# A two-part model in one fp32 kernel: start, modulation rows, scan outputs and gated heads rearranged

## The chip, the cores and the metric

The kernel runs on one core of a Trainium2 chip. The metric is the time of one execution on the device in microseconds (us); lower is better. All matrix products are fp32.

## The reference, cut to what matters

256 tokens of width 1024 go through a first block (two layers: projection, convolution, windowed attention, layer norms; a dense feed-forward in layer 0, eight experts with two chosen a token in layer 1), and then through a second block of two layers with attention and a two-directional recurrent scan. What the change touches:

```python
h = layer_norm(x, ln_in_g, ln_in_b)                       # the start
mod_x = split(silu(c) @ w_ada[l] + b_ada[l], 3)           # modulation rows, c and c_ctx: 2 rows
mod_c = split(silu(c_ctx) @ w_ada[l] + b_ada[l], 3)
# the scan, per chunk of 128 tokens, for 4 heads and 2 directions
num = w_inter * (C @ q) + qk @ v
h = num / max(abs(den), exp(-m_t))                        # output of a chunk
C = a * C + (w * v) @ k                                   # state change
# the gated heads
h = rmsnorm(sigmoid(o_pre) * h) * head_g * silu(z)
out = concat([att, h]) @ w_out
```

## The kernel before, in words

Activations lie feature-major (128 features on the partitions, 8 chunks, 256 tokens along the free axis). TensorE (PE) does all products, VectorE (DVE) and ScalarE (ACT) what lies between, SyncE (SP) starts every transfer. Each engine has its own instruction list in program order, written out by hand in `build`; semaphores join them. Weights arrive as units of 1 MB (`next_unit`), into a ring of six slots before the experts; SP loads a unit as soon as PE has released the slot. PSUM has eight banks: `fill` makes PE wait until the last reader of a bank is done, `tile` makes a reader wait until PE has filled it.

The start. SP (lines 1521 to 1523) starts a transfer of the first constants (ones, identity, zeros and small ones), of the tokens `x_t` into `xc`, and of the parameters. PE waits for the constants, does two products of 128x512 whose results nobody reads (`spin(2)`), waits for the tokens, and sums them over the features with the matrix of ones (`norm_mean`); DVE subtracts the mean (L2090), ACT squares (L1597), PE sums the squares (`norm_var`), ACT takes the root (L1583), DVE scales (L2104, L2121) and PE takes up the projections after `spin(3)`.

The modulation rows. `w_ada` has 12 units a layer. For each, `condition_rows` or `condition_row` multiplies the two conditions, padded to 32 columns, with the unit's eight feature chunks: 16 fp32 products of 128x32 weights in 4 column groups of PE for every two units, chunk c in group c % 4, so that a row is spread over four groups of partitions. ACT copies the bank, and `condition_turns` (by `turn`) sums the four parts and turns them to feature-major with products against two columns of the constant `fold`: 2 of them a unit, 4 for two units. Ten of these pairs stand in the rounds of the first block's attention (`block1_attention`: six in layer 0, four in layer 1), where the order of each round is: scores, values of the round before, rows, half of the output projection, turns, transposes of the softmax (L689). Four units, two pairs, stand beside the norm at the end of layer 0 (`norm_beside_conditions`).

The scan (`mlstm`, on PE and on DVE). There are four steps j, in each both directions d. PE does for a step: scores of both directions, `inter(j,0)`, `state_change(j,0)`, `inter(j,1)`, `intra(j,0)`, `state_change(j,1)`, `intra(j,1)`, with pieces of projections between them (`mlstm_beside_projections`). `inter` and `intra` of both directions use the same two banks, 5 and 6: `intra(j,1)` waits until DVE's `output(j,0)` has taken its sum out of them (L2804, semaphore `mh_num`). DVE's own order in a step ends with `state_change(j,0)`, `state_change(j,1)` (L2792), `output(j,0)`, `output(j,1)` (L2804 to L2819). In layer 0 all four steps have outputs, in layer 1 the last two; the last step has no state change.

The gated heads (`mlstm_post` on DVE, `mlstm_turn`, `block2_out_start` and `block2_out` on PE). After the norm, PE transposes the heads of each tile of 128 tokens (L1429, 4 tiles in layer 0, 2 in layer 1, a bank each), and DVE multiplies each 128x128 piece by the gate (L2872 in layer 0, tile by tile; L2863 in layer 1, head by head). In layer 0 PE then waits for all four tiles before the second half of the output product; in layer 1 it waits head by head, and does the first half of another column chunk before that.

Of the kernel before, what the change touches and what calls it, by code (L numbers as in the profile page):

```python
# [14 lines left out]
P = 128  # L15
T = 256
# [162 lines left out]
def const_columns():  # L179
    c = Columns()  # L180
    for name, n in (("ones", P), ("ident", P), ("zeros", P), ("tri_f", P), ("eps5", 1), ("eps6", 1), ("one", 1), ("fold", COL),
                    ("tri_b", P), ("mask_f", P), ("mask_b", P), ("rot", P), ("cos", T), ("sin", T), ("win_mask", TT * 2 * T), ("slot", BIG), ("capacity", EXPERTS), ("bases", EXPERTS),
                    ("nbr_mask", TT * T), ("before", EXPERTS * EXPERTS)):
        c.add(name, n)
    c.early = c.at["eps5"][0] + 3 + COL
    return c
# [5 lines left out]
def build(nc, weights, params, consts, x_t, ctx_t, p_t, rel, out, rows_dram):  # L192
    with ExitStack() as ctx:
# [58 lines left out]
        row_of = (cond_row, other_row)  # L252
# [78 lines left out]
        names = """weights_used ones_loaded x_loaded params_loaded late_loaded rel_loaded rel_ready out_stored  # L331
# [118 lines left out]
        def _(eng):  # L450
# [32 lines left out]
            def spin(n):  # L483

                for _ in range(n):
                    mm(ps[:, 7, :], ones, con[:, 0:512], True, True)
# [94 lines left out]
            def row_products(l, u, o):  # L581
                w = next_unit()
                for c in range(KC):
                    at = 32 * (c % 4)
                    last = mm(o[at:at + 32, 0:GW], cond_s[:, c, :], w[:, c * GW:(c + 1) * GW], c < 4, c >= KC - 4)
                return last

            def condition_row(l, u, bank):
                o = fill(("row", l, u), bank, (s["cond_row"], UNITS_ADA * l + u + 1))
                row_products(l, u, o).then_inc(bank_full[bank], 1)  # L590

            def turn(u, rows, mod_t):
                for half in range(2):
                    at = 2 * (2 * u + half)
                    last = mm(mod_t[:, at:at + 2], rows[:, u % 2, half * P:half * P + P],
                              con[:, CN("fold", 0, 2)], True, True)
                return last

            def condition_turn(l, u, mod_t):
                eng.wait_ge(s["cond_row"], UNITS_ADA * l + u + 1)  # L600
                return turn(u, cond_row, mod_t)

            def condition_rows(l, n, beside=False):

                u = l * ADA_EARLY + 2 * n
                bank = 1 if n else 5
                o = fill(("row", l, u), bank, (s["cond_row"], UNITS_ADA * l + u + 2))
                for k in range(2):
                    w = next_unit(beside=beside or k == 1)
                    for c in range(KC):  # L610
                        at = 32 * (c % 4)
                        last = mm(o[at:at + 32, k * GW:(k + 1) * GW], cond_s[:, c, :], w[:, c * GW:(c + 1) * GW],
                                  c < 4, c >= KC - 4)
                last.then_inc(bank_full[bank], 1)

            def condition_turns(l, n, mod_t):
                u = l * ADA_EARLY + 2 * n
                eng.wait_ge(s["cond_row"], UNITS_ADA * l + u + 2)
                for k in range(2):
                    last = turn(u + k, row_of[n % 2], mod_t)  # L620
                if u + 2 == UNITS_ADA:
                    last.then_inc(bank_full[0], 1)

            def norm_beside_conditions():
# [8 lines left out]
                condition_row(1, 2, 7)  # L633
                condition_row(1, 3, 4)
                condition_turn(1, 2, mod_t)
                condition_turn(1, 3, mod_t).then_inc(bank_full[5], 1)
# [787 lines left out]
            def mlstm_turn(l):  # L1424
                eng.wait_ge(s["mh_normed"], l + 1)
                for t in range(4 if l == 0 else 2):
                    o = fill(("mt", l, t), t, (s["mh_mixed"], 8 if l else t + 1))
# [4 lines left out]
            def out_half(l, w, c, o, half):  # L1432
                alone = l == 1 and c >= CC
                n = 2 * T if l == 0 else T
                for k in range(CC * half, CC * half + CC):
                    if l == 1 and c == 0 and half == 1:
                        eng.wait_ge(s["mh_mixed"], 4 + k - CC + 1)
# [20 lines left out]
            def block2_out(l, started):  # L1458
                if l == 0:
                    eng.wait_ge(s["mh_mixed"], 4)  # L1460
# [116 lines left out]
        def _(eng):  # L1577
# [26 lines left out]
            def condition_row(l, u):  # L1604
                o = tile(eng, "row", l, u)
                eng.activation(cond_row[:, u % 2, :], o[:, 0:GW], ACT.Copy).then_inc(s["cond_row"], 1)

            def condition_rows(l, n):
                u = l * ADA_EARLY + 2 * n
                o = tile(eng, "row", l, u)  # L1610
                eng.activation(row_of[n % 2].rearrange("p a b -> p (a b)"), o, ACT.Copy).then_inc(s["cond_row"], 2)
# [417 lines left out]
            eng.wait_ge(s["ones_loaded"], 16)  # L2029
            norm("in", KC, T)  # L2030
            eng.wait_ge(s["params_loaded"], 16)
            eng.wait_ge(s["prep_done"], 1)
            eng.activation(cond_s[:, :, 0:2], par[:, PC.all("cond")].rearrange("p (c e) -> p c e", e=2), ACT.Silu)\
                .then_inc(s["cond_ready"], 1)
            for l in range(DEPTH):
# [11 lines left out]
                else:  # L2047
                    ffn()
                    condition_row(1, 0)
# [1169 lines left out]
```

## Time and profile before

| | us |
|---|---|
| median of 3 runs | 2022.15 (2021.82 to 2023.66) |
| the profiled execution, its own time | 2021.61 |
| its span, first to last instruction | 2019.8 |
| PE busy | 1979.9 (98%) |
| DVE busy | 754.0 (37%) |
| ACT busy | 404.1 (20%) |

The span of 2019.8 us lies within an execution of 2021.61 us; 1.8 us lie around it. An instruction row of the trace gives its start and its duration in us from the span's start, the engine, the line in the kernel, what it writes and reads, and how many instructions were merged; in brackets the idle time of the engine before it and what ended it. A fp32 product shows as two MATMUL records, a transpose as one. Ends of products are modelled, so durations of a merged row reach past the start of the next: pitch is read from starts. Rows of a view by shape give the count, then busy time, mean ns of one, and idle time before.

### The profile page before, as it was taken

How to read it: one execution, taken by the hardware profiler on the slowest of the kernel's cores; microseconds unless marked ns; L12 is line 12 of the kernel's file. 1: busy time of each engine (PE TensorE's matmuls, PEld its weight loads, DVE VectorE, ACT ScalarE, POOL GpSimd, SP SyncE). 2: the span in 40 equal slices, each digit the busy share in tenths (PEclk: the TensorE clock that was granted, in tenths of full speed). 3: DMA queues.
4: the chain of work that ended last, by engine and by line, in shares of the span. 5: the costliest groups of instructions: out<-in, count | busy, mean ns of one | idle time of the engine just before them, and what ended most of it. 6: DMA issues, size and time to landing. Idle time of an engine off the chain costs nothing.

```text
span 2019.8 us, 36525 instructions
## 1 busy us (share of the span) xinstructions
PE 1979.9 (98%) x15702; PEld 1439.5 (71%) x15702; DVE 754.0 (37%) x1781; ACT 404.1 (20%) x947; POOL 0.2 (0%) x4
## 2 busy tenths in 40 slices
PE   9999999999999999999999999999999999999998
PEld 7879999988766656666656666656755667566787
DVE  6847555587521111111111111111326823426725
ACT  1233110114310111000100010000214432223342
POOL 0000000000000000000000000000000000000000
PEclk9999999999999999999999999999999999999999
DMA  9473645455199999999999999999132111122220
GB/s 337 167 287 129 211 172 193 174 188 188 63 402 420 421 419 421 420 420 420 420 421 420 420 416 420 420 420 421 71 112 87 52 63 42 63 103 85 105 84 22
DMA packets 75826, 510.94 MB, mean 253 GB/s; under 512 B 7888, under 2 KB 14096, under 8 KB 14992
## 3 DMA queue, kind: packets, MB, share of 16 engines
q1 hardware_dynamic: 75664, 508.58, 63.0%
q8 instruction: 126, 2.06, 0.4%
q14 instruction: 36, 0.29, 0.0%
HBM read 507.46 MB, written 1.08 MB: 252 GB/s over the span
## 4 chain that ended last, share of the span: by engine, by line
PE 92%; DMA 4%; DVE 2%; ACT 1%; issue 1%; SPq 0%; DVEq 0%; ACTq 0%
PE ps L477 90%; DMA ring<-weights 3%; DMA work<-weights 1%; PE ps L1269 1%; PE ps L818 1%; PE ps L689 0%; SPq L1534 0%; DVE work L2872 0%; DVE work L2792 0%; DVE spare L2725 0%; DMA con<-consts 0%; DVE work L2116 0%; ACT work L1597 0%; DVE work L2804 0%; DVE small L2908 0%
## 5 line engine op out<-in xcount | busy, mean ns | idle before, releaser
L477 PE MATMUL ps<-work 128*32 128x256 f32 (+8 forms) x4912 | 516.6, 375 | 10.7 <-DVE work L2804 6.3
L477 PE MATMUL ps<-work,ring 128*128 128x256 f32 (+2 forms) x1992 | 503.7, 407 | 3.1 <-DVE work L2872 3.1
L477 PEld LDWEIGHTS ps<-work 128*32 128x32 f32 (+3 forms) x4912 | 345.3, 142 | 142.2 <-issue 77.0
L477 PEld LDWEIGHTS ps<-work,ring 128*128 128x128 f32 x1992 | 340.0, 191 | 137.5 <-issue 108.5
L477 PE MATMUL ps<-ring,work 128*32 128x256 f32 (+3 forms) x4392 | 405.8, 407 | 3.6 <-DMA ring<-weights 3.0
L477 PEld LDWEIGHTS ps<-ring,work 128*32 128x32 f32 (+1 forms) x4392 | 234.1, 120 | 130.2 <-issue 59.7
L477 PE MATMUL ps<-xc,ring 128*128 128x256 f32 (+1 forms) x1344 | 252.3, 348 | 0.0
L477 PEld LDWEIGHTS ps<-xc,ring 128*128 128x128 f32 x1344 | 222.7, 191 | 31.0 <-issue 5.1
L2378 DVE TENSOR_TENSOR work<-work,ps 128x256 f32<-128x256 f32 x42 | 17.7, 421 | 413.2 <-ACT work L1745 413.2
L1745 ACT ACTIVATE work<-ps 128x256 f32<-128x256 f32 x42 | 16.1, 384 | 557.8 <-PE ps L477 557.8
L477 PE MATMUL ps<-spare,work 128*32 128x256 f32 (+1 forms) x1128 | 120.4, 427 | 2.1 <-issue 1.2
L477 PE MATMUL ps<-xc,work 128*128 128x256 f32 (+1 forms) x624 | 117.2, 346 | 0.0
L477 PEld LDWEIGHTS ps<-xc,work 128*128 128x128 f32 x624 | 102.7, 191 | 16.3 <-issue 4.2
L2153 DVE SCALAR_TENSOR_TENSOR work<-work,par 128x256 f32<-128x256 f32 x240 | 98.0, 479 | 0.9
L2341 DVE TENSOR_TENSOR work<-ps,work 128x512 f32<-128x512 f32 x68 | 47.0, 691 | 92.4 <-PE ps L477 92.1
L477 PEld LDWEIGHTS ps<-spare,work 128*32 128x32 f32 x1128 | 52.2, 110 | 37.9 <-issue 21.2
L477 PE MATMUL ps<-work,con 128*128 128x256 f32 x230 | 55.4, 385 | 8.5 <-ACT work L1597 4.3
L477 PEld LDWEIGHTS ps<-work,con 128*128 128x128 f32 x230 | 42.2, 190 | 20.2 <-issue 8.2
L2499 DVE TENSOR_TENSOR work<-ring 128x512 f32<-128x512 f32 x52 | 33.6, 687 | 53.4 <-PE ps L477 53.4
L2392 DVE TENSOR_TENSOR work<-work 128x512 f32<-128x512 f32 x14 | 9.7, 692 | 97.6 <-ACT work L1751 97.6
L477 PE MATMUL ps<-xc,spare 128*128 128x256 f32 x192 | 42.7, 381 | 0.0
L477 PEld LDWEIGHTS ps<-xc,spare 128*128 128x128 f32 x192 | 36.2, 190 | 7.3 <-issue 1.7
(287 smaller groups left out, 1267.0 us busy)
## 6 DMA issues: line engine op xcount, KB each, us to landing
ring<-weights SPq DMA_DIRECT2D x287, 1024.0 KB, 15.0
work<-weights SPq DMA_DIRECT2D x130, 1024.0 KB, 20.3
spare<-weights SPq DMA_DIRECT2D x54, 1024.0 KB, 19.9
work<-rel SPq DMA_DIRECT2D x8, 512.0 KB, 13.6
spare<-rows SPq DMA_DIRECT2D x2, 2048.0 KB, 9.3
con<-consts SPq DMA_DIRECT2D x1, 1368.0 KB, 21.6
xc<-x_t SPq DMA_DIRECT2D x1, 1024.0 KB, 5.7
xc<-ctx_t SPq DMA_DIRECT2D x1, 1024.0 KB, 27.0
```

The source lines that it names most:

```text
L477: ins = eng.matmul(o, lhs, rhs, start=start, stop=stop, **kw)
L818: last = eng.transpose(o[:, k * P:k * P + P], pair_a[:, n % 2, k * P:k * P + P], ident)
L1269: last = eng.transpose(o[:, kt * P:kt * P + P], prob2_flat[:, at:at + P], ident)
L1745: eng.activation(pair_s[:, n % 2, :], o[:, 0:GW], ACT.Silu).then_inc(s["pair_silu"], 1)
L2153: ins = eng.scalar_tensor_tensor(out=conv_acc[:, j, :], in0=src, scalar=w, in1=conv_acc[:, j, :], op0=ALU.mult, op1=ALU.add)
L2341: return eng.tensor_tensor(r, o.rearrange("p (a b) -> p a b", b=T), r, ALU.add)
L2378: eng.tensor_tensor(pair_a[:, n % 2, :], pair_s[:, n % 2, :], o[:, GW:2 * GW], ALU.mult)\
L2392: eng.tensor_tensor(v, v, rows(gate_row, 2), ALU.mult).then_inc(s["first_weighted"], 1)
L2499: ins = eng.tensor_tensor(up_sum(i, z), in0, in1, op)
```

## The change

- The tokens are the first transfer, into the contiguous buffer `res` instead of `xc`; the constants follow without the ones, which DVE writes by a memset. PE waits for that memset alone, and its idle products are 12, 3 and 6 of 128x128 instead of 2 and 3 of 128x512.
- Modulation rows go in pairs of units. Each pair puts one unit into column groups 0 and 1 and the other into 2 and 3 (`fold2` has four columns), fills 256 instead of 512 columns of one bank, is copied by one ACT instruction, and is turned by 2 products of four columns instead of 4 of two. Both units are waited for at the pair's first product.
- In the scan DVE does `output(j,0)` before `state_change(j,1)`.
- The gated heads are one DVE operation a head over all tiles (4 for a layer), after all transposes, and in layer 0 too PE waits head by head.

```diff
+    for name, n in (("ones", P), ("ident", P), ("zeros", P), ("tri_f", P), ("eps5", 1), ("eps6", 1), ("one", 1), ("fold", COL), ("fold2", 4),
...
+            def condition_rows(l, n, bank=None, beside=False):
+
+                u = l * ADA_EARLY + 2 * n
+                if bank is None:
+                    bank = 1 if n else 5
+                o = fill(("row", l, u), bank, (s["cond_row"], (UNITS_ADA * l + u) // 2 + 1))
+                w = [next_unit(beside=beside), next_unit(beside=True)]
+                for c in range(0, KC, 2):
+                    for k in range(2):
+                        for j in range(2):
+                            at = 64 * k + 32 * j
+                            last = mm(o[at:at + 32, 0:GW], cond_s[:, c + j, :], w[k][:, (c + j) * GW:(c + j + 1) * GW],
+                                      c == 0, c == KC - 2)
+                last.then_inc(bank_full[bank], 1)
...
+            def condition_turns(l, n, mod_t):
+
+                u = l * ADA_EARLY + 2 * n
+                eng.wait_ge(s["cond_row"], (UNITS_ADA * l + u) // 2 + 1)
+                to = mod_t[:, 4 * u:4 * u + 8].rearrange("p (k a e) -> p k a e", k=2, a=2)
                 for half in range(2):
...
+                    last = mm(to[:, :, half, :], row_of[n % 2][:, half * P:half * P + P], con[:, CN.all("fold2")],
+                              True, True)
...
-                condition_row(1, 0, 7)
-                condition_row(1, 1, 4)
+                condition_rows(1, -2, 7)
                 norm_mean("ln2_0", res, KC, T)
                 mod_t = fill(("mod_early",), 5, (s["mod_out"], 2))
-                condition_turn(1, 0, mod_t)
-                condition_turn(1, 1, mod_t)
+                condition_turns(1, -2, mod_t)
                 norm_var("ln2_0", KC, T, True)
...
+                condition_rows(1, -1, 4)
+                condition_turns(1, -1, mod_t).then_inc(bank_full[5], 1)
...
-            eng.wait_ge(s["ones_loaded"], 16)
-            spin(2)
+            eng.wait_ge(s["prep_done"], 1)
+            spin(12)
             eng.wait_ge(s["x_loaded"], 16)
-            norm("in", xc, KC, T)
+            norm_mean("in", res, KC, T)
             spin(3)
+            norm_var("in", KC, T, True)
+            spin(6)
+            eng.wait_ge(s["consts_loaded"], 16)
...
+                    if c == 0 and half == 1:
+                        eng.wait_ge(s["mh_mixed"], 4 * l + k - CC + 1)
...
+            eng.memset(ones, 1.0).then_inc(s["prep_done"], 1)
...
-            eng.dma_start(con[:, 0:CN.early], consts[:, 0:CN.early]).then_inc(s["ones_loaded"], 16)
-            eng.dma_start(xc[:, :, 0:T], x_t).then_inc(s["x_loaded"], 16)
+            eng.dma_start(res, x_t).then_inc(s["x_loaded"], 16)
+            eng.dma_start(con[:, P:CN.early], consts[:, P:CN.early]).then_inc(s["consts_loaded"], 16)
...
                     if j < 3:
                         state_change(j, 0)
+                    if row_work:
+                        output(j, 0)
+                    if j < 3:
                         state_change(j, 1)
                     if row_work:
-                        output(j, 0)
                         output(j, 1)
...
                 for t in range(tiles):
+                    tile(eng, "mt", l, t)
+                for h in range(M_HEADS):
+                    to, gates = (v[:, 0:tiles * P].rearrange("p (a b) -> p a b", b=P)
+                                 for v in (mix2[CC + h], mzs[:, h, :]))
+                    eng.scalar_tensor_tensor(out=to, in0=ps[:, 0:tiles, h * P:h * P + P],
+                                             scalar=par[:, PC(f"head_g{l}", h)], in1=gates,
+                                             op0=ALU.mult, op1=ALU.mult).then_inc(s["mh_mixed"], 1)
```

On PE, at the program's start (`con` holds the ones, `xc` and `res`, which is part of `work`, the tokens). Before:

```order
L477 MATMUL ps<-con 128x512 [waits ones_loaded]
L477 MATMUL ps<-con 128x512
L477 MATMUL ps<-xc,con 128x256 [waits x_loaded]
L477 MATMUL ps<-xc,con 128x256 x7
L477 MATMUL ps<-work,con 128x256 [waits norm_squared] x8
L477 MATMUL ps<-con 128x512 x3
```

And in the change:

```order
L477 MATMUL ps<-con 128x128 [waits prep_done]
L477 MATMUL ps<-con 128x128 x11
L477 MATMUL ps<-work,con 128x256 [waits x_loaded]
L477 MATMUL ps<-work,con 128x256 x7
L477 MATMUL ps<-con 128x128 x3
L477 MATMUL ps<-work,con 128x256 [waits norm_squared] x8
L477 MATMUL ps<-con 128x128 x6
```

The first product no longer waits for a transfer, and idle products stand before and after the sum of squares.

On PE, in the first block's attention, the rows and turns of a round (`ring` holds the units, `con` the columns of `fold`). Before:

```order
L477 MATMUL ps<-ring,work 32x256 [waits weights_in3,cond_row]
L477 MATMUL ps<-ring,work 32x256 x7
L477 MATMUL ps<-ring,work 32x256 [waits weights_in4]
L477 MATMUL ps<-ring,work 32x256 x7
L477 MATMUL ps<-work,ring 128x256 [waits mix_biased]
L477 MATMUL ps<-work,ring 128x256 x7
L477 MATMUL ps<-con,work 128x2 [waits cond_row]
L477 MATMUL ps<-con,work 128x2 x3
```

And in the change:

```order
L477 MATMUL ps<-ring,work 32x256 [waits weights_in3,weights_in4,cond_row]
L477 MATMUL ps<-ring,work 32x256 x15
L477 MATMUL ps<-work,ring 128x256 [waits mix_biased]
L477 MATMUL ps<-work,ring 128x256 x7
L477 MATMUL ps<-con,work 128x2x2 [waits cond_row]
L477 MATMUL ps<-con,work 128x2x2
```

The 16 row products stay, both units are waited for ahead of them, and two of the four turns are gone.

On DVE, in the first step of the scan in layer 0 (`state_change` writes 128x129 pieces of the state, `output` begins with the 128x516 sum). Before:

```order
L2792 SCALAR_TENSOR_TENSOR work<-work,ps 128x129 x8
L2804 TENSOR_TENSOR work<-ps,work 128x516
L2809 SCALAR_TENSOR_TENSOR work<-work 128x4
L2811 TENSOR_TENSOR work<-work 128x4
L2812 RECIPROCAL work<-work 128x4
L2816 TENSOR_TENSOR work<-work 128x512
L2804 TENSOR_TENSOR work<-ps,work 128x516
```

And in the change:

```order
L2768 SCALAR_TENSOR_TENSOR work<-work,ps 128x129 x4
L2780 TENSOR_TENSOR work<-ps,work 128x516
L2785 SCALAR_TENSOR_TENSOR work<-work 128x4
L2787 TENSOR_TENSOR work<-work 128x4
L2788 RECIPROCAL work<-work 128x4
L2792 TENSOR_TENSOR work<-work 128x512
L2768 SCALAR_TENSOR_TENSOR work<-work,ps 128x129 x4
L2780 TENSOR_TENSOR work<-ps,work 128x516
```

The first direction's output stands ahead of the second direction's state change.

## Rows read from the trace of the kernel before

**Rows 1.** Page, the chain that ended last: shares of the span by engine.

```profile
PE 92%; DMA 4%; DVE 2%; ACT 1%; issue 1%; SPq 0%; DVEq 0%; ACTq 0%
```

**Rows 2.** Waits of PE, 24 to 533 us: total, times, longest (us).

```profile
PE ps L477 <- ACT work L1597: 1.4, 2, 1.1
PE ps L477 <- DVEq L2613: 0.7, 1, 0.7
```

**Rows 3.** Waits of PE, 1640 to 2021 us.

```profile
PE ps L477 <- DVE work L2804: 6.3, 4, 1.6
```

**Rows 4.** PE in order of time, 2 to 20 us.

```profile
3.73 3.78 PE L477 MATMUL ps<-con 128*128 128x512 f32 x4 [3.73 <-DMA con<-consts]
7.31 4.71 PE L477 MATMUL ps<-xc,con 128*128 128x256 f32 x16
...
16.62 2.74 PE L477 MATMUL ps<-con 128*128 128x512 f32 x6
```

**Rows 5.** All engines in order of time, 0 to 30 us.

```profile
0.74 0.39 SPq L1521 DMA_DIRECT2D con<-consts  x1
1.19 0.66 SPq L1522 DMA_DIRECT2D xc<-x_t  x1
...
12.13 2.74 DVE L2090 SCALAR_TENSOR_TENSOR work<-ps,xc 128x256 f32<-128x256 f32 x8 [12.13 <-PE ps L477]
...
15.16 0.27 DVE L2975 MEMSET work<- 128x256 f32 x1
```

**Rows 6.** Transfers, 0 to 12 us: KB each, us from issue to landing.

```profile
xc<-x_t SPq DMA_DIRECT2D x1, 1024.0 KB, 5.7
```

**Rows 7.** Windows: busy us of PE, PEld, DVE, ACT, POOL; clock; DMA share; GB/s.

```profile
8.00:9.00 1.00, 1.00 (x3) 0.74 (x3) 0.00 (x0) 0.00 (x0) 0.00 (x0) 1.00 1.02 424
...
519.00:534.00 15.00, 14.11 (x65) 11.75 (x63) 6.64 (x17) 0.24 (x1) 0.00 (x0) 1.00 0.03 12
...
1744.00:1745.00 1.00, 1.00 (x2) 0.48 (x3) 0.00 (x0) 0.00 (x0) 0.00 (x0) 0.50 0.00 0
```

**Rows 8.** PE in order of time, one attention round of layer 0.

```profile
101.86 0.95 PE L477 MATMUL ps<-con,work 128*128 128x2 f32 x8
102.67 1.07 PE L689 MATMUL ps<-con,work 128*128 128x128 f32 x8
```

**Rows 9.** PE by shape, 90 to 520 us: the turns of twelve pairs.

```profile
L477 PE MATMUL ps<-con,work 128*128 128x2 f32 x96 | 12.0, 246 | 0.0
```

**Rows 10.** ACT in order of time, the same round of attention.

```profile
102.06 0.84 ACT L1692 ACTIVATE work<-ps,par 128x256 f32<-128x256 f32 x2 [1.12 <-PE ps L477]
```

**Rows 11.** Transfers of weights, 92 to 132 us.

```profile
ring<-weights SPq DMA_DIRECT2D x10, 1024.0 KB, 6.0
```

**Rows 12.** PE in order of time, end of the scan's first step, layer 0.

```profile
1654.23 1.05 PE L477 MATMUL ps<-work 128*128 128x129 f32 x8
1655.12 3.60 PE L477 MATMUL ps<-work,ring 128*128 128x512 f32 x8
1658.56 1.06 PE L477 MATMUL ps<-work 128*128 128x129 f32 x8
1661.18 1.13 PE L477 MATMUL ps<-work 128*128 128x129 f32 x8 [1.56 <-DVE work L2804]
1662.15 3.60 PE L477 MATMUL ps<-work,ring 128*128 128x512 f32 x8
```

**Rows 13.** DVE in order of time, the same stretch.

```profile
1659.31 1.12 DVE L2792 SCALAR_TENSOR_TENSOR work<-work,ps 128x129 f32<-128x129 f32 x4 [8.41 <-PE ps L477]
1660.35 0.69 DVE L2804 TENSOR_TENSOR work<-ps,work 128x516 f32<-128x516 f32 x1
```

**Rows 14.** PE in order of time, the gated heads of layer 0.

```profile
1738.79 1.91 PE L1429 MATMUL ps<-con,work 128*128 128x128 f32 x16
1743.78 42.99 PE L477 MATMUL ps<-work,ring 128*128 128x512 f32 x96 [3.09 <-DVE work L2872]
```

**Rows 15.** DVE in order of time, the gated heads of layer 0.

```profile
1739.50 4.23 DVE L2872 SCALAR_TENSOR_TENSOR work<-ps,par,work 128x128 f32<-128x128 f32 x16 [0.94 <-PE ps L1429]
```

More of the change, by code:

```diff
@@ L184, in const_columns @@
         c.add(name, n)
-    c.early = c.at["eps5"][0] + 3 + COL
+    c.early = c.at["eps5"][0] + 3 + COL + 4
     return c
@@ L485, in spin @@
                 for _ in range(n):
-                    mm(ps[:, 7, :], ones, con[:, 0:512], True, True)
+                    mm(ps[:, 7, 0:P], ones, ones, True, True)
             def norm(name, src, chunks, n, centred=True, bank=0):
@@ L579, in block1_projection @@
                 norm_var(f"conv{l}", CC, T, True, 2)
[L581 to L603, printed above, removed]
-                u = l * ADA_EARLY + 2 * n
[L606 to L613, printed above, removed]
+            def condition_rows(l, n, bank=None, beside=False):
+                u = l * ADA_EARLY + 2 * n
+                if bank is None:
[8 more added lines that the diff above has]
+                                      c == 0, c == KC - 2)
                 last.then_inc(bank_full[bank], 1)
@@ L1426, in mlstm_turn @@
                 for t in range(4 if l == 0 else 2):
-                    o = fill(("mt", l, t), t, (s["mh_mixed"], 8 if l else t + 1))
+                    o = fill(("mt", l, t), t, (s["mh_mixed"], 4 * l + 4))
                     for h in range(M_HEADS):
@@ L1610, in condition_rows @@
                 o = tile(eng, "row", l, u)
-                eng.activation(row_of[n % 2].rearrange("p a b -> p (a b)"), o, ACT.Copy).then_inc(s["cond_row"], 2)
+                eng.activation(row_of[n % 2], o[:, 0:GW], ACT.Copy).then_inc(s["cond_row"], 1)
             def context_squares():
@@ L2027, in mlstm_std @@
                 inverse_root(rms_i[:, 0:n], rms_s[:, 0:n], "eps6", M_DH).then_inc(s["mh_std"], 1)
-            eng.wait_ge(s["ones_loaded"], 16)
-            norm("in", KC, T)
+            norm_squares("in", KC, T)
+            eng.wait_ge(s["consts_loaded"], 16)
+            norm_std("in", KC, T)
             eng.wait_ge(s["params_loaded"], 16)
-            eng.wait_ge(s["prep_done"], 1)
+            eng.wait_ge(s["prep_done"], 2)
             eng.activation(cond_s[:, :, 0:2], par[:, PC.all("cond")].rearrange("p (c e) -> p c e", e=2), ACT.Silu)\
@@ L2048, in _ @@
                     ffn()
[L2049 to L2050 removed]
+                    condition_rows(1, -2)
                     norm("ln2_0", KC, T)
[L2052 to L2053 removed]
+                    condition_rows(1, -1)
             norms_beside_context()
@@ L2976, in prepare @@
                 clear_margins().then_inc(s["prep_done"], 1)
-                eng.wait_ge(s["prep_done"], 1)
+                eng.wait_ge(s["prep_done"], 2)
+            eng.memset(ones, 1.0).then_inc(s["prep_done"], 1)
             eng.wait_ge(s["x_loaded"], 16)
-            norm("in", xc, KC, T, layer_gain("ln_in_g", "ln_in_b", xc), beside=prepare)
+            norm("in", res, KC, T, layer_gain("ln_in_g", "ln_in_b", xc), beside=prepare)
             for l in range(DEPTH):
@@ L3173, in const_tile @@
     t[:, CN.all("fold")] = i[:, None] % COL == np.arange(COL)[None, :]
+    t[:, CN.all("fold2")] = (i[:, None] // 64 == np.arange(4) // 2) & (i[:, None] % COL == np.arange(4) % 2)
     t[:, CN.all("slot")] = np.arange(BIG)[None, :]
```

41 lines of the change are left out of this document (4 added, 37 removed).

## The prediction, made before the changed kernel ran

> **What bounds the kernel now.** I read the page first. Its chain that ended last is PE for 92% of the span [rows 1], so a microsecond is worth a microsecond only if PE stops working or waiting for it. Next I read the waits of PE in the stages that the change touches. From 24 to 533 us, where the modulation rows lie, PE waits three times, for 2.1 us in all, and never for a transfer [rows 2]: there only fewer PE instructions help. After 1640 us, in the second block, it waits four times for DVE's L2804, 6.3 us in all [rows 3], and once, for 3.1 us, for the gated heads [rows 14]. Last I read the start in order of time: PE's first product comes at 3.73 us, when the constants have landed, and DVE begins with the tokens at 12.13 us [rows 4, 5]. The experts in the middle are fed by transfers, but these begin behind the routing: between 519 and 534 us the transfer engines are 3% busy [rows 7]. What is won ahead of the routing therefore shifts the experts as a whole.
>
> **The start.** Four products of 128x512 (four records) take 3.78 us at first and six records 2.74 us later [rows 4], 0.95 against 0.46 us each. The clock column reads 1.00 in the slow stretch too [rows 7], but the durations are those of the lower level, 1.2 GHz, first and of 2.4 GHz later. Per record of 128x256 that is about 0.43 and 0.215 us (the second is half of 3.44 / 8 us, the pitch of a 128x512 record in [rows 12]). The 16 records of the sum over the tokens take 4.71 us [rows 4]: x slow and 16 - x fast ones with a tail of 0.17 us give x = 5. So PE rose some 5.7 us after it began at 3.73 us. In the change PE waits only for a memset of DVE. The earliest instruction behind the common barrier is at 0.74 us [rows 5], and a memset of twice the size takes 0.27 us [rows 5], so PE begins near 1.1 us. The 12 idle products are 24 records at 0.21 to 0.24 us (half of a slow 128x256 record; twice the 1.91 / 16 us of a fast 128x128 one [rows 14]) and end at 6.5 to 7.1 us. The tokens are now issued at 0.74 instead of 1.19 us; with the 5.7 us of [rows 6] they land at 6.4 us. The sum then begins near 6.8 us instead of 7.31 us, and if PE rises 5.7 us after its start, at 6.8 us, all 16 records are fast: 3.45 + 0.17 us, and DVE starts at 10.5 instead of 12.13 us. I take **1.5 us**. Bounds: 2.6 us, if the clock follows PE's start by the whole 2.6 us and the idle products speed up before their end; and a loss of 1.3 us (first rival). The rest of the start hangs on DVE and moves along: the new 3 and 6 idle products lie in waits that were there, the constants land long before ACT's root needs them, and the removed long idle products only held up a product that DVE paces.
> The Trainium skill, "TensorE: Matmul & The Clock Gate", Part 1, says that the clock's rise costs a span of time under load and not a number of products; by that rule thin products serve as well, and the sum keeps its 1.5 us, while without it the first rival's loss stands. The Trainium skill, "DMA: Bandwidth & Descriptors", section Bandwidth, gives 6.15 us for a transfer of 1 MB; by that, which speaks against the reordering, the tokens land at an estimated 6.9 us and the sum is 0.2 us smaller.
>
> **The modulation rows.** The 16 row products of a pair stay, in four column groups as before: nothing. The turns shrink from 8 records to 4. Eight take 0.81 us from start to start [rows 8], so each pair saves 0.405 us. There are 96 such records before, twelve pairs [rows 9]. Ten pairs lie in attention rounds, where PE does not wait: **4.05 us**. Two lie beside a norm, where PE waits for ACT and DVE before and after [rows 2]: nothing, at most 0.8 us. Cover: the transposes behind the turns now come 0.4 us earlier, and their first copy on ACT needs ACT free from L1692, which ends at 102.06 + 0.84 = 102.90 us [rows 10]; the first bank of transposes would be full at 102.67 - 0.4 + 0.5 = 102.8 us. It just fits; where it does not, some 0.1 us a round comes back, so the low bound is 3.0 us. ACT copies half as much in the pair's copy, off the path.
> The new wait is for both units ahead of a pair's first product. Behind it on PE stands everything else. A unit lands 6.0 us after its issue [rows 11] and is issued several units ahead, and PE never waited for one [rows 2]; asking for the second one eight row products earlier costs nothing. If that lead were gone, see the third rival.
>
> **The scan.** `intra(0,0)` ends about 1655.2 us, and DVE then idles: 8.41 us before 1659.31 us [rows 12, 13]. But it does the second state change first, and takes the sum out of banks 5 and 6 only at 1660.35 to 1661.04 us, so that `intra(0,1)` starts at 1661.18 instead of right behind the records of 1658.56 us [rows 12, 13]. In the new order the sum is out by 1656 us. The 16 records from 1658.56 to 1662.15 us take 3.59 us; at the pitch of the eight from 1654.23 to 1655.12 us they take 1.78 us [rows 12]. That is 1.8 us a time, and four such waits stand in the trace [rows 3], three in layer 0 and one in layer 1: **7.2 us**. The four idle times alone, 6.3 us [rows 3], are the low bound if all else holds. What DVE does earlier is an output of five instructions, six in odd steps; even at 0.69 us for each of them, the first one's time [rows 13], five end at 1658.9 us, ahead of the state change at 1659.31 us, and six 0.3 us behind it, for which nobody waits before the next step. Next late would be the scores and projections of PE itself.
>
> **The gated heads.** In layer 0 DVE works from 1739.50 to 1743.73 us and PE stands until 1743.78 us [rows 14, 15]. In the change DVE waits for all 16 transposes, to about 1740.85 us, then writes a head of 128x512 in 0.69 us (as L2804, 128x516 from PSUM [rows 13]); PE goes on at 1741.6 us, and its first product a head (two records of 0.43 us) is longer than DVE's 0.69 us. That is 2.2 us. Second, the clock: it reads 0.50, the lower of the two levels, at 1744 to 1745 us [rows 7], behind 3.09 us without a product, and the 96 records take 42.99 us [rows 14] where 96 x 0.43 + 0.17 = 41.45 us are due. With a gap of 0.9 us I expect no fall: 1.55 us more, **3.75 us** together. In layer 1 PE has other products ahead of the heads and waits head by head already: nothing.
> The same page of the Trainium skill, Part 1, says that the moment of a change of clock differs from run to run; by it some executions before may not have paid the 1.55 us, and the median would then gain 2.2 us here. The profiled one paid it, so I keep 3.75 us and put 2.2 us into the range.
>
> **Sum.** 1.5 + 4.05 + 7.2 + 3.75 = 16.5 us against the profiled execution's own 2021.61 us, whose span is 2019.8 us: 2005.1 us. The median of the runs is 0.54 us above that execution, so I forecast **2005.7 us**.
>
> **Rivals.**
> 1. The thin idle products do not raise the clock, and the sum over the tokens pays for the rise. From 6.8 us, 13 records at 0.43 us and 3 at 0.215 us end at 13.2 us instead of 12.0 us: a loss of 1.3 us instead of the 1.5 us. 2022.15 - 13.7 = 2008.5 us. For it: the trace has no stretch of 128-column products on a slow clock. Against it: PE is just as busy. Chance 0.12.
> 2. The scan's wait is halved, not gone, since DVE or ACT comes late for another step (keys, scaled sums): 3.6 us instead of 7.2 us, 2009.3 us. Against it: DVE idles for 8.41 us in that step [rows 13]. Chance 0.08.
> 3. Slower: PE waits in each of the twelve pairs for the second unit. A whole unit costs 1 MB at the 424 GB/s of [rows 7], 2.5 us; twelve of them 30 us, and 2022.15 - 16.5 + 30 = 2035.7 us. It decides when the wait is more than 20.5 / 12 = 1.7 us a pair, that is, when a unit is issued less than some 5 us ahead of its pair. Against it: [rows 2]. Chance 0.02.
> 4. The first half's gain is given back by the experts, if their transfers do not shift: 16.5 - 5.55 = 11 us, 2011.2 us. Against it: the idle transfer engines of [rows 7]. Chance 0.05. That nothing of the change arrives (banks or semaphores hold each engine where it was) would give 2022 us; chance 0.03.
>
> **The numbers.** The forecast has 0.70. Its bounds reach from 18.4 us (2.6, 4.85, 7.2, 3.75) to 12.5 us (1.0 at the start, 3.0, 6.3, 2.2), 2003.75 to 2009.65 us. The range takes in rivals 1, 2 and 4 and, below, the 0.33 us by which the lowest run shown lies under the median: 2003.3 to 2011.4 us. A measurement can tell some 0.2%, 4 us, from no change: below 2018.1 us lie the forecast, rivals 1, 2 and 4, so faster 0.95; rival 3 is slower 0.02; same 0.03.
>
> **What would show it.** Right: DVE's first subtraction near 10.5 us; the turns' count halved and 0.4 us between turns and transposes; no wait of PE for the 128x516 sum; about 0.9 us of waiting at the gated heads of layer 0 and no 0.50 in the clock behind it. Wrong: any wait of PE for weights between 24 and 533 us, slow records after 8 us at the start, or a new wait of PE for `intra` or `inter`.

## The result, and the profile after

| | before | after |
|---|---|---|
| median, us | 2022.78 (4 runs, 2021.82 to 2023.66) | 2003.12 (4 runs, 2002.64 to 2003.49) |
| profiled execution, us | 2021.61 | 2002.64 |
| its span, us | 2019.8 | 2000.9 |

The ratio is 0.9903 [0.9886, 0.992]: faster by 19.7 us between the medians and by 18.97 us between the two profiled executions. The sum forecast 16.5 us, and 2003.12 us lies 0.2 us below the low end of the range.

The page of the changed kernel, first the busy times, then the chain that ended last:

```profile
PE 1972.6 (99%) x15686; PEld 1437.2 (72%) x15686; DVE 752.6 (38%) x1766; ACT 401.2 (20%) x945; POOL 0.2 (0%) x4
...
PE 93%; DMA 4%; DVE 1%; ACT 1%; issue 0%; SPq 0%; DVEq 0%; ACTq 0%
```

PE was busy for 7.3 us less (1979.9 us before), and the other 11.6 us of the span are time in which it stood; the chain is even more PE's than in [rows 1]. All engines in order of time, 0 to 13 us, of the changed kernel (start, us, engine, line, operation; answers to [rows 4, 5]):

```profile
0.74 0.39 SPq L1502 DMA_DIRECT2D work<-x_t  x1
...
1.06 5.32 PE L477 MATMUL ps<-con 128*128 128x128 f32 x24 [1.06 <-DVE con L2947]
...
6.21 3.62 PE L477 MATMUL ps<-work,con 128*128 128x256 f32 x16
...
9.95 2.74 DVE L2066 SCALAR_TENSOR_TENSOR work<-ps,work 128x256 f32<-128x256 f32 x8 [8.95 <-PE ps L477]
```

PE begins at 1.06 instead of 3.73 us, all 16 records of the sum are fast, and DVE begins 2.18 us earlier. PE in order of time in the same attention round as [rows 8], and PE by shape, 90 to 520 us (answers to [rows 9]):

```profile
99.28 0.51 PE L477 MATMUL ps<-con,work 128*128 128x4 f32 x4
99.65 1.07 PE L669 MATMUL ps<-con,work 128*128 128x128 f32 x8
```
```profile
L477 PE MATMUL ps<-con,work 128*128 128x4 f32 x48 | 6.6, 243 | 0.5 <-ACT work L1588 0.5
```

Half as many turns, 0.37 us a pair instead of 0.81. Waits of PE, 24 to 526 us, which ends at the same place in the program as the 533 us of [rows 2] (total, times, longest; answers to [rows 2]):

```profile
PE ps L477 <- ACT work L1578: 1.8, 2, 1.1
PE ps L477 <- DVEq L2589: 0.7, 1, 0.7
PE ps L477 <- ACT work L1588: 0.5, 1, 0.5
```

There is still no wait for weights. Beside the norm, where two pairs take less of PE's time, it stands longer for ACT instead (1.8 us instead of 1.4, and 0.5 us for the rows' copy). Waits of PE, 1630 to 2001 us (answers to [rows 3]):

```profile
PE ps L477 <- DVE work L2915: 1.2, 2, 0.6
PE ps L477 <- DVE work L2841: 1.0, 1, 1.0
```

No row for the 128x516 sum (now L2780) is left; the heads cost 1.0 instead of 3.1 us. First step of the scan in layer 0, PE and then DVE in order of time (answers to [rows 12, 13]):

```profile
1646.51 1.06 PE L477 MATMUL ps<-work 128*128 128x129 f32 x8
1647.40 3.60 PE L477 MATMUL ps<-work,ring 128*128 128x512 f32 x8
1650.84 1.95 PE L477 MATMUL ps<-work 128*128 128x129 f32 x16
1652.62 3.60 PE L477 MATMUL ps<-work,ring 128*128 128x512 f32 x8
```
```profile
1647.66 0.70 DVE L2780 TENSOR_TENSOR work<-ps,work 128x516 f32<-128x516 f32 x1 [4.49 <-PE ps L477]
...
1651.58 1.13 DVE L2768 SCALAR_TENSOR_TENSOR work<-work,ps 128x129 f32<-128x129 f32 x4 [1.89 <-PE ps L477]
```

The sum now leaves the banks at 1648.4 us, 3.2 us ahead of the second state change, and the 16 records of 128x129 run through in 1.78 us. The gated heads of layer 0: PE, then DVE, then a window behind them (busy us of PE, PEld, DVE, ACT, POOL; clock; DMA share; GB/s; answers to [rows 14, 15, 7]):

```profile
1725.65 1.91 PE L1409 MATMUL ps<-con,work 128*128 128x128 f32 x16
1728.52 41.47 PE L477 MATMUL ps<-work,ring 128*128 128x512 f32 x96 [0.95 <-DVE work L2841]
```
```profile
1727.71 2.73 DVE L2841 SCALAR_TENSOR_TENSOR work<-ps,par,work 128x512 f32<-128x512 f32 x4 [2.28 <-PE ps L1409]
```
```profile
1729.00:1730.00 1.00, 1.00 (x4) 0.47 (x3) 1.00 (x3) 0.00 (x0) 0.00 (x0) 1.00 0.00 0
```

Four operations of 0.68 us take the place of sixteen; PE needs only the first of them, its stop is 0.95 us, and the clock stays at 1.00. The table takes the steps between starts of the same instructions, in us; the last four columns are the experiments with one part each.

| step | before | after | start | rows | scan | heads |
|---|---|---|---|---|---|---|
| span's start to DVE's first subtraction | 12.13 | 9.95 | 9.50 | 12.48 | 12.28 | 11.56 |
| rows and rounds of layer 0 | 42.78 | 40.10 | 42.78 | 40.10 | 42.78 | 42.78 |
| from there to the end of the norm with two pairs beside it | 272.20 | 272.19 | 272.20 | 272.20 | 272.20 | 272.20 |
| rows and rounds of layer 1 | 37.40 | 35.61 | 37.40 | 35.61 | 37.40 | 37.41 |
| routing to the norm behind the experts | 876.96 | 875.84 | 876.61 | 876.70 | 876.66 | 876.89 |
| scan of layer 0, to the transposes | 96.66 | 91.25 | 96.66 | 96.65 | 91.25 | 96.65 |
| transposes to the first head's product | 4.99 | 2.87 | 5.00 | 5.00 | 5.00 | 2.86 |
| from there to the norm (96 records) | 43.60 | 42.07 | 43.77 | 42.08 | 45.00 | 42.08 |
| scan of layer 1, to the transposes | 66.25 | 64.45 | 66.25 | 66.25 | 64.46 | 66.25 |
| from there to DVE's last operation | 19.63 | 19.27 | 19.28 | 19.64 | 19.62 | 19.28 |

### The profile page after: what moved, and what is told of

It is laid out like the page before. It is cut to its first block, busy times and chain, and to the rows that moved or that the text cites. A ratio compares the mean times of both kernels' runs of the same rounds, so it can differ in the third digit from the quotient of the medians.

```text
span 2000.9 us, 36477 instructions
## 1 busy us (share of the span) xinstructions
PE 1972.6 (99%) x15686; PEld 1437.2 (72%) x15686; DVE 752.6 (38%) x1766; ACT 401.2 (20%) x945; POOL 0.2 (0%) x4
## 4 chain that ended last, share of the span: by engine, by line
PE 93%; DMA 4%; DVE 1%; ACT 1%; issue 0%; SPq 0%; DVEq 0%; ACTq 0%
PE ps L477 91%; DMA ring<-weights 3%; DMA work<-weights 1%; PE ps L1249 1%; PE ps L798 1%; PE ps L669 0%; DVE spare L2701 0%; DVE work L2092 0%; ACT work L1578 0%; PE ps L1409 0%; DVE small L2876 0%; ACT work L1889 0%; DVE work L2873 0%; SPq L1515 0%; PE ps L1363 0%
## 6 DMA issues: line engine op xcount, KB each, us to landing
work<-weights SPq DMA_DIRECT2D x130, 1024.0 KB, 19.7
```

## The experiments

**One part at a time.** Four kernels carry one part of the change each; they were measured beside 25 runs of the kernel before with a median of 2022.15 us.

The start:

```diff
-            eng.wait_ge(s["ones_loaded"], 16)
-            spin(2)
+            eng.wait_ge(s["prep_done"], 1)
+            spin(12)
...
-            eng.dma_start(con[:, 0:CN.early], consts[:, 0:CN.early]).then_inc(s["ones_loaded"], 16)
-            eng.dma_start(xc[:, :, 0:T], x_t).then_inc(s["x_loaded"], 16)
+            eng.dma_start(res, x_t).then_inc(s["x_loaded"], 16)
+            eng.dma_start(con[:, P:CN.early], consts[:, P:CN.early]).then_inc(s["consts_loaded"], 16)
```

> The kernel before with the new start alone. Theory (the parts add up, and the 1.1 us that the experts were shorter in the changed kernel's profile is scatter of their transfers): DVE's first subtraction near 9.95 us as in the changed kernel, 2.2 us earlier than before, all 16 records of the sum over the tokens fast; time 2.2 us less, give or take the scatter of the experts, with waits of PE for transfers there between 4.5 and 6 us. Rival (the experts gain because everything ahead of them comes earlier): the waits for transfers in the experts shrink by about a third of the 1.1 us here, as the start is a third of what comes ahead of them.

Measured: 2018.64 us, ratio 0.9979 [0.997, 0.9989], 3.5 us by the medians. DVE begins at 9.50 us, earlier than expected, and what lies behind it moves along. PE's waits for transfers in the experts were 3.9 us, outside the 4.5 to 6 us of the theory and shorter by more than the rival's third of 1.1 us; the step of the experts itself was 0.35 us shorter.

The rows (`condition_rows` and `condition_turns` as in the change):

```diff
-                    last = mm(mod_t[:, at:at + 2], rows[:, u % 2, half * P:half * P + P],
-                              con[:, CN("fold", 0, 2)], True, True)
+                    last = mm(to[:, :, half, :], row_of[n % 2][:, half * P:half * P + P], con[:, CN.all("fold2")],
+                              True, True)
```

> The kernel before with the modulation rows in pairs alone. Theory: the stretch from the start of the first projections to the routing is 4.4 us shorter (0.44 us for each of ten pairs, nothing for the two beside the norm), no wait of PE for a weight unit there; time 4.4 us less. Rival (as forecast, 0.405 us a pair): 4.05 us. Second rival (the experts gain with the shift): the waits of PE for transfers in the experts are 0.7 us shorter than the 5.7 us of before.

Measured: 2017.35 us, ratio 0.9977 [0.9968, 0.9987], 4.8 us. The two stretches with rows are 2.68 and 1.79 us shorter, 4.47 us for ten pairs; the pairs beside the norm bring nothing.

The scan:

```diff
                         state_change(j, 0)
-                        state_change(j, 1)
                     if row_work:
                         output(j, 0)
+                    if j < 3:
+                        state_change(j, 1)
+                    if row_work:
                         output(j, 1)
```

> The kernel before with the other order of the scan's outputs alone. Theory: no wait of PE for the sum out of banks 5 and 6 (before: four, 6.3 us); the scan of layer 0 is 5.4 us and that of layer 1 1.8 us shorter; time 7.2 us less. Rival (half of it returns as a wait for keys or scaled sums): 3.6 us less, and a new wait of PE for DVE or ACT between 1640 and 1740 us.

Measured: 2014.48 us, ratio 0.9959 [0.9945, 0.9973], 7.7 us. The scan of layer 0 is 5.41 us shorter and that of layer 1 1.79 us: 7.20 us, or 1.80 us for each of the four waits.

The heads:

```diff
+                for h in range(M_HEADS):
...
+                    eng.scalar_tensor_tensor(out=to, in0=ps[:, 0:tiles, h * P:h * P + P],
+                                             scalar=par[:, PC(f"head_g{l}", h)], in1=gates,
+                                             op0=ALU.mult, op1=ALU.mult).then_inc(s["mh_mixed"], 1)
```

> The kernel before with one operation a head alone. Theory (the shorter stop spares the fall of the clock too): PE's stop at the gated heads of layer 0 falls from 3.1 to 1.0 us, the clock reads 1.00 behind it, and the 96 records of the output product take 41.5 instead of 43.0 us; time 3.7 us less. Rival (the clock falls for another reason, at a moment of its own): 2.2 us less, and 0.50 in the clock somewhere in the output product.

Measured: 2017.74 us, ratio 0.9979 [0.9969, 0.9989], 4.4 us. The stop is 2.13 us shorter and the 96 records take 42.08 us.

What follows from the four: alone they win 3.5 + 4.8 + 7.7 + 4.4 = 20.4 us by medians with 2 to 3 us of doubt each, together 19.7 us; the parts do not get in each other's way. The table shows each step moving only where its part stands, with four exceptions that no edit there explains: the start (11.56 to 12.48 us with the old start), the experts, the 96 records (42.08 to 45.00 us with the old heads) and the last stretch (19.28 or 19.63 us). PE's waits for weights in the experts, 520 to 1440 us, were 5.7 us in the profile of before, 4.6 after, and 3.9, 5.3, 3.7 and 4.1 us in these four; the shortest belongs to the scan's kernel, in which nothing ahead of the experts differs from before. So these waits scatter by 2 us without any edit. They don't say how long the step is, though: a second profile of the kernel before (below) has 4.1 us of them instead of 5.7, and its step of the experts is 876.91 instead of 876.96 us. The next runs went to the start and to the 96 records.

**The clock at the heads.** Behind the stop of the kernel with the scan's part alone, PE in order of time and a window:

```profile
1738.23 44.39 PE L477 MATMUL ps<-work,ring 128*128 128x512 f32 x96 [3.09 <-DVE work L2874]
```
```profile
1738.00:1739.00 1.00, 0.77 (x1) 0.50 (x2) 0.17 (x1) 0.00 (x0) 0.00 (x0) 0.50 0.00 0
...
1744.00:1745.00 1.00, 1.00 (x3) 0.38 (x2) 0.11 (x1) 0.00 (x0) 0.00 (x0) 0.93 0.00 0
```

The clock is down when PE resumes and up again only after 1744 us: 2.9 us lost, where before lost 1.5 and the kernel with the rows alone nothing, all three with the same stop of 3.09 us. To see whether the stop is the cause, it was made long again in the changed kernel.

```diff
                 for t in range(tiles):
                     tile(eng, "mt", l, t)
+                if l == 0:
+                    link(eng.tensor_tensor(o2, o2, o2, ALU.add))
```

> The changed kernel with one more DVE instruction (an addition of 128x2048 to itself, which changes the outputs) ahead of the first gated head of layer 0, so that PE stands there for some 3.2 us again instead of about 1. Theory (the length of the stop decides about the clock): besides the added 2.3 us in the step from the last transpose to the first product of the heads, the 96 records behind it take more than their 42.07 us, by 0 to 2.9 us (the four runs with the old stop took 42.08 to 45.00), and the profile reads 0.50 in its clock column there whenever they do; 2005.4 to 2008.3 us. Rival (the fall has to do with the order of DVE's work or with what lies ahead, not with the stop): the records stay at 42.07 us, no 0.50, and only the 2.3 us are paid, 2005.4 us.

Measured: 2006.85 us, ratio 0.9929 [0.9912, 0.9945]; single runs of 2005.58, 2005.56, 2008.19 and 2008.12 us. The profiled one (2005.58 us) showed 42.07 us and no fall, as the rival has it; but the four runs lie on two levels 2.6 us apart, as the theory would have it if the upper two paid for a fall, which no profile of them shows. So the same kernel was profiled twice more, and once with a second such addition.

> The kernel with the 3.3 us stop at the heads once more. Of four profiles with a stop of 3.1 us three showed a fall of the clock (1.5 to 2.9 us lost in the 96 records), this kernel's first profile with 3.3 us none, and five with 0.95 us none. Theory (a stop of 3 us makes the clock fall in some executions and not in others): at least one of this run and the next shows 43.5 us or more for the 96 records and 0.50 in the clock. Rival (the fall needs something else of the old order): 42.07 us in both.

> As the run ahead of it, the third profile of the same kernel: theory 43.5 us or more in at least one of the two, rival 42.07 us in both.

```diff
                     link(eng.tensor_tensor(o2, o2, o2, ALU.add))
+                    link(eng.tensor_tensor(o2, o2, o2, ALU.add))
```

> As the run ahead of it with a second such DVE addition, so that PE stands for some 5.6 us at the first heads. Theory (the length of the stop decides): the clock falls, the 96 records take 43.5 to 45.5 us; 2009.5 to 2011.5 us. Rival: 42.07 us, 2008 us.

PE at the heads in the three profiles of the 3.3 us stop and in that of the longer one:

```profile
1731.28 41.47 PE L477 MATMUL ps<-work,ring 128*128 128x512 f32 x96 [3.27 <-DVE work L2843]
```
```profile
1731.07 43.16 PE L477 MATMUL ps<-work,ring 128*128 128x512 f32 x96 [3.27 <-DVE work L2843]
```
```profile
1732.09 41.47 PE L477 MATMUL ps<-work,ring 128*128 128x512 f32 x96 [3.27 <-DVE work L2843]
```
```profile
1733.85 43.22 PE L477 MATMUL ps<-work,ring 128*128 128x512 f32 x96 [5.60 <-DVE work L2844]
```

And a window behind the stop in the second of them:

```profile
1732.00:1733.00 1.00, 1.00 (x3) 0.48 (x2) 0.99 (x2) 0.00 (x0) 0.00 (x0) 0.50 0.00 0
```

Measured: steps of 42.07, 43.78 and 42.07 us for the same kernel, and 43.83 us (2010.1 us, one run) for the longer stop. The theory holds: behind a stop of 3.1 to 3.3 us the clock fell in some executions (five of eight profiles) and not in others, behind a stop of 0.95 us in none of five (42.07 or 42.08 us each). The Trainium skill, "TensorE: Matmul & The Clock Gate", Part 1, says that the moment of a change, there of the rise at a start, differs from run to run; the 42.07 and 43.78 us of one program agree with it.

**The start.** Two kernels take the new start apart, beside the changed kernel itself. Without the first idle products:

```diff
             eng.wait_ge(s["prep_done"], 1)
-            spin(12)
             eng.wait_ge(s["x_loaded"], 16)
```

> The changed kernel without the 12 idle products ahead of the sum over the tokens; the memset and the early issue of the tokens stay. Theory (the thin idle products raised the clock): PE begins when tokens and constants have landed, near 6 us, the records of the sum are slow (0.43 us each) and DVE's first subtraction comes at 12.5 to 13.5 us instead of 9.95; 2005.8 to 2006.8 us against 2003.1. Rival (they raise nothing, the clock is up by itself by then): the sum takes 3.8 us as in the changed kernel, DVE begins at 9.5 to 10 us and the time is that of the changed kernel. The start of the sum also shows when the tokens really land, which the idle products hide: under 6.2 us if they are the bound in the changed kernel.

PE, then DVE, in order of time in that kernel:

```profile
5.77 6.57 PE L477 MATMUL ps<-work,con 128*128 128x256 f32 x16 [5.77 <-DMA work<-x_t]
```
```profile
12.46 0.76 DVE L2065 SCALAR_TENSOR_TENSOR work<-ps,work 128x256 f32<-128x256 f32 x2 [11.46 <-PE ps L477]
```

Measured: 2005.73 us (2004.85 to 2006.35), ratio 0.992 [0.9904, 0.9937], 1.9 us more than the changed kernel beside it. The sum takes 6.57 instead of 3.6 us and DVE begins at 12.46 us, both times just below the theory's ranges, and 3.0 us later than in the changed kernel beside it. The tokens land in time for PE at 5.77 us. The theory holds: with the 24 thin records of 128 columns ahead of it the sum is fast, without them it is slow.

With the old order of the two transfers:

```diff
-            eng.dma_start(res, x_t).then_inc(s["x_loaded"], 16)
             eng.dma_start(con[:, P:CN.early], consts[:, P:CN.early]).then_inc(s["consts_loaded"], 16)
+            eng.dma_start(res, x_t).then_inc(s["x_loaded"], 16)
```

> The changed kernel with its first two transfers in the old order again: constants ahead of tokens on SP's queue. Separates the two halves of the new start. Theory (the early idle products, not the tokens' place in the queue, win most of the start): the tokens land some 0.5 us later, the sum starts at 6.2 to 6.8 us instead of 6.2 and stays fast; 2003.1 to 2003.7 us. Rival (the tokens' place is what counts): the sum starts at 7.3 us or later as before, 1 us or more is lost, 2004.2 us or more.

PE in order of time, then the transfer (KB, us from issue to landing) in that kernel:

```profile
6.11 3.72 PE L477 MATMUL ps<-work,con 128*128 128x256 f32 x16 [0.53 <-DMA work<-x_t]
```
```profile
work<-x_t SPq DMA_DIRECT2D x1, 1024.0 KB, 4.9
```

Measured: 2003.72 us (2003.52 to 2004.01), ratio 0.9911 [0.9894, 0.9927], no difference from the changed kernel beside it. The tokens' place in the queue brings nothing that can be measured at this start: they land 0.3 us later (6.11 against 5.77 us in the kernel ahead), and DVE begins at 9.95 us as in the first profile of the change.

> The changed kernel itself once more, beside the others and as their measure. Its median should come at 2003.1 us within 1 us. If the experts' waits for transfers are scatter (3.7 to 5.7 us in the six profiles so far), they lie in that range here too and not always at 4.6; the records behind the heads should take 42.07 us again, with no 0.50 in the clock.

Measured: 2003.83 us (2002.97 to 2004.06), ratio 0.9912 [0.9895, 0.9928]; DVE's subtraction at 9.48 us, 42.08 us behind the heads, 4.8 us of waits for weights in the experts. All as expected.

> The kernel before, profiled once more: what of its first profile is particular to that execution. If the profile of before was taken in a slow draw, the step from DVE's first subtraction to the first layer is shorter than 12.13 us (11.5 to 12.5 us in the five old starts and two profiles of them), the 96 records behind the heads take 42.08 to 45.0 us, the experts 876.2 to 877.0 us, and the last stretch 19.28 or 19.63 us.

The kernel before once more, its transfer of the tokens and then PE and DVE in order of time:

```profile
xc<-x_t SPq DMA_DIRECT2D x1, 1024.0 KB, 7.7
```
```profile
8.92 5.34 PE L477 MATMUL ps<-xc,con 128*128 128x256 f32 x16 [1.39 <-DMA xc<-x_t]
...
14.39 2.74 DVE L2090 SCALAR_TENSOR_TENSOR work<-ps,xc 128x256 f32<-128x256 f32 x8 [14.39 <-PE ps L477]
```

Measured: 2023.97 us, one run. The start was expected at 11.5 to 12.5 us and came at 14.39: the tokens landed at 8.9 us, and PE stood 1.39 us for them. The other steps were in their ranges (43.78 us behind the heads, 876.91 us for the experts, 19.62 us at the end). So the first profile of before was no long execution, as this expectation held possible; its start was an early one.

None of these kernels beat the changed one by an amount that can be measured, and the experiments point to no version that would.

## Why the prediction was right in kind and short in size

All four mechanisms arrived, none of the rivals did. Between the two profiles the sum is 2.5 us short: 0.7 us at the start, 0.4 us in the modulation rows, and 1.5 us in two stages that the prediction put at nothing, the experts (1.1 us) and the last stretch (0.4 us); the heads came 0.1 us below their term. By the steps of the sum:

| term | forecast | between the two profiles | elsewhere |
|---|---|---|---|
| start | 1.5 | 2.2 | 2.7 between the means of 5 and 8 profiles |
| modulation rows | 4.05 | 4.47 | 4.47 with the rows alone |
| scan | 7.2 | 7.2 | 7.2 with the scan alone |
| heads, the stop | 2.2 | 2.1 | 2.1 with the heads alone |
| heads, the clock | 1.55 | 1.5 | 0 to 2.9, 1.6 on average of 5 profiles |
| experts and last stretch | 0 | 1.1 + 0.4 | see below |
| sum | 16.5 | 19.0 | |

- **The start is the term of the change that was mis-sized.** The step that failed reads: "The sum then begins near 6.8 us". It began at 6.21 us, and its own length was right (3.74 us to DVE's start). The 6.8 us lie in the middle of "end at 6.5 to 7.1 us", but 24 records at 0.21 to 0.24 us from 1.1 us end at 6.1 to 6.9 us. They ended at 6.21 us, and PE went on without a wait for the tokens; so it was in six of the eight profiles with idle products, and in the other two PE waited 0.46 and 0.53 us for the tokens. (In the same paragraph the four records of 3.78 us are two products, not four.) The clock's rise came within the idle products or at their end in six of these eight; in two it came a little into the sum (3.98 and 4.00 us from the sum's start to DVE's, instead of 3.74 to 3.84).
  A second fault lies beside it: "with the 5.7 us of [rows 6] they land at 6.4 us." Had that been so, the sum could not have begun before 6.4 us, so 0.4 of the 0.6 us come from the idle products' end alone and 0.2 us needed earlier tokens. In the profile of the change they took 5.0 us and landed at 5.7 us; over nine profiles of the new start it was 4.8 to 5.2 us. (The 6.15 us that the prediction takes from the Trainium skill, "DMA: Bandwidth & Descriptors", section Bandwidth, is a figure for transfers that GpSimd issues; here SP issues them.) The 5.7 us belonged to another transfer: `x_t` into `xc`. The change also moves the destination to the contiguous `res`, which its description tells but the prediction did not price. In five profiles of the old transfer it took 5.7, 6.5, 7.2, 7.4 and 7.7 us. Place in the queue is not the reason, since with the constants ahead it still took 4.9 us. What is left is the destination, and the 64 KB of ones that the constants lost, an estimated 0.15 us at the 424 GB/s of [rows 7]. The packets of the first 12 us, of before and of the change, fit this:

```profile
DMA packets 1538, 3.81 MB, mean 318 GB/s; under 512 B 64, under 2 KB 1088, under 8 KB 1344
```
```profile
DMA packets 671, 3.99 MB, mean 332 GB/s; under 512 B 64, under 2 KB 192, under 8 KB 320
```

  Under 8 KB there are 1024 packets fewer, one for each KB of the tokens. No run moved the tokens to `res` alone, so the share of the packets in the 0.5 to 2.9 us between the two forms is argued, not shown.
- **The modulation rows** were 0.4 us short. "Eight take 0.81 us from start to start [rows 8], so each pair saves 0.405 us" halves the time; four turns of four columns take 0.37 us, so a pair saves 0.44 to 0.45. The ten pairs counted and the two beside the norm did not (272.20 us before, 272.19 after), as forecast; the doubt whether ACT would be late for the transposes cost nothing.
- **The scan and the heads' stop** came within 0.1 us of their terms. The reading that carried the scan was the idle time of DVE ahead of its state change [rows 13]: the sum was ready to be taken, and only the order of a list kept it.
- **The clock at the heads** came as forecast between these two profiles, and the runs show that it varies from execution to execution: of five profiles of the old order four lost 1.5 to 2.9 us and one lost nothing. The prediction named this for one side of its range only (2.2 instead of 3.75 us); a loss of 2.9 us before, which makes the gain larger, stood in no bound.
- **The experts and the last stretch** were put at nothing and brought 1.5 us between the two profiles. For the experts the step reads: "What is won ahead of the routing therefore shifts the experts as a whole." Their step lies at 876.6 to 877.0 us in six profiles with at least three parts undone, and at 875.8 to 876.8 us in eight with all or nearly all of the change; the means are 0.5 us apart. No single part shortens it by more than 0.35 us. So some 0.5 of the 1.1 us may be the change's, and the rest lies within the scatter of either group; how the change would do it stays open.
  The last stretch has two levels, 19.28 and 19.63 us. It stood at the upper one in both profiles of before and in those of the rows and of the scan alone, at the lower one in all ten others, which carry the new start or the new heads. The difference is the idle time of DVE ahead of its last operations, between the end of ACT's root and DVE's first scaling (before, then after):

```profile
2013.93 3.25 DVE L2116 SCALAR_TENSOR_TENSOR work<-xc,par,work 128x256 f32<-128x256 f32 x8 [2.17 <-ACT work L1583]
```
```profile
1994.97 3.25 DVE L2092 SCALAR_TENSOR_TENSOR work<-xc,par,work 128x256 f32<-128x256 f32 x8 [1.81 <-ACT work L1564]
```

  The four profiles at the upper level are also the ones in which DVE has exactly as many instructions as before (1781 on the page; 1765 to 1768 or 1782 in the others). So this looks like an effect of the change and not like scatter, but what makes DVE start later was not tested.
- **The range** was too narrow below because its low end was a sum of bounds on the change's own terms, with none for the stages behind it, plus the 0.33 us by which three runs scattered (2003.75 less 0.33 is 2003.42 us; the 2003.3 us stated are 0.1 us more generous). The kernel before spreads from 2019.31 to 2025.09 us over all its runs here, and its profiles show two things that differ from execution to execution: DVE's start (11.56 to 14.39 us) and the 96 records behind the heads (42.08 to 45.00 us). In the eight profiles with the change's start and its idle products the first lies within 9.48 to 10.34 us, in the five with its heads the second is 42.07 or 42.08 us, and the eight runs of the changed kernel spread only from 2002.64 to 2004.06 us.

## What to carry to other kernels

Where one engine is the bound and stands still for another that idles ahead of the operation waited for, the order of that other engine's list is a cheap thing to change, and its worth could be read here to a tenth of a microsecond from the two timelines (7.2 us forecast and measured). A stop of PE of 3 us cost more than its length in some executions, so shortening such a stop may save the clock's fall as well; price the term by several profiles, not by the value of one. When a transfer changes its destination, its old time from issue to landing need not hold, even if the bytes are the same. And a stage that the change doesn't touch can move too, here by up to 1.1 us between two profiles; a range needs room for it.

## What the runs showed of the hardware that was not expected

- The same stop of PE (3.27 us), in the same program, was followed by 42.07 us or by 43.78 us for the same 96 records. With the stop of 3.09 us the fall came while PE stood in one profile (scan alone, 2.9 us lost), and while it stood or after it had resumed in others (1.5 to 1.7 us lost). A stop of 5.6 us cost 1.8 us, less than one of 3.09 us had once.
- The 1 MB of tokens landed in 4.8 to 5.2 us where each partition takes its 8 KB in one piece (`res`), and in 5.7 to 7.7 us where it takes eight pieces of 1 KB (`xc`). The second form scattered by 2.0 us, the first by 0.4. The two also differ in the constants' size and in the time that SP takes to issue them (0.39 or 0.42 against 0.66 or 0.67 us), so the pieces are not shown to be the reason.
